# Weights of q, k and v of the third scan in three fp32r products, u's parts kept in one place, and both directions of a second-scan level in one VectorE instruction

## What is computed

```python
u = rmsnorm(h, norm_mix_g[l])
(s_z, s_xbc, s_dt, g_q, g_f, g_i, g_g, m_q, m_k, m_v, m_i, m_f, m_o, gates) = split(u @ w_in[l])
y_ssd = ssd_branch(s_z, s_xbc, s_dt)            # first scan, 16 heads, both directions
y_hg  = hgrn2_branch(g_q, g_f, g_i, g_g)        # second scan, 8 heads of 128 channels, both directions
y_ml  = mlstm_branch(m_q, m_k, m_v, m_i, m_f, m_o)   # third scan, 8 heads, both directions
merged = gate0 * (y_ssd @ w_br_ssd) + gate1 * (y_hg @ w_br_hg) + gate2 * (y_ml @ w_br_ml)
h = h + merged @ w_out
u = rmsnorm(h, norm_ffn_g[l]);  h = h + (silu(a) * v) @ w_down      # a, v from a convolution of u @ w_up
h = h + (p @ w_ple) * sigmoid(h @ w_ple_gate)
```

## Time and profile before

| | us |
|---|---|
| median of 3 runs (lowest, highest) | 2100.21 (2099.66, 2102.2) |
| span of the profiled execution, first to last instruction | 2098.0 |
| TensorE matmuls busy | 1965.0 (94%) |
| VectorE busy | 1271.7 (61%) |
| ScalarE busy | 932.0 (44%) |
| POOL busy | 31.4 (1%) |

### The profile page before, as it was taken

The page is one execution under the profiler, slowest core; times in us unless marked ns, Lnnn a source line. Parts: engine busy times, 40 slices in busy tenths (PEclk is TensorE's granted clock), DMA queues, the critical chain, the costliest instruction groups (busy, mean ns, idle before and its releaser), DMA issues.

```text
span 2098.0 us, 45360 instructions
## 1 busy us (share of the span) xinstructions
PE 1965.0 (94%) x19452; PEld 1719.3 (82%) x19452; DVE 1271.7 (61%) x2183; ACT 932.0 (44%) x1166; POOL 31.4 (1%) x62
## 2 busy tenths in 40 slices
PE   8999999999999999999999999999999996777776
PEld 7998869999999999988689999999977764444444
DVE  6887879489688567896895796786435311111111
ACT  5544655574565445546455754664422310111011
POOL 0000000000000000000000000000000000000000
PEclk9999999999999999999999999999999998999988
DMA  6555344445455554654434544555777899999997
GB/s 238 183 206 188 130 161 143 170 181 187 167 183 184 205 184 160 218 202 147 176 129 154 201 161 163 186 186 190 264 321 277 353 427 429 429 428 429 429 429 318
DMA packets 60269, 498.86 MB, mean 238 GB/s; under 512 B 7152, under 2 KB 7280, under 8 KB 12240
## 3 DMA queue, kind: packets, MB, share of 16 engines
q1 hardware_dynamic: 54864, 479.57, 59.5%
q0 software_dynamic: 4384, 14.49, 2.1%
q10 hardware_dynamic: 864, 2.49, 0.4%
HBM read 495.38 MB, written 1.15 MB: 237 GB/s over the span
## 4 chain that ended last, share of the span: by engine, by line
PE 72%; DMA 15%; DVE 8%; ACT 3%; issue 1%; ACTq 0%; SPq 0%; DVEq 0%
PE bank L1063 28%; DMA arena<-stream 15%; PE bank L1068 14%; PE bank L1073 4%; PE bank L1670 3%; PE bank L1051 3%; PE bank L1357 3%; PE bank L1002 3%; PE bank L990 2%; PE bank L1056 1%; DVE ring_r L2742 1%; PE bank L1105 1%; PE bank L1704 1%; PE bank L1649 1%; PE bank L1460 1%
## 5 line engine op out<-in xcount | busy, mean ns | idle before, releaser
L2742 DVE TENSOR_TENSOR ring_r<-ring,weights_and_u_split 128x2048 fp32r<-128x2048 f32 x88 | 201.5, 2291 | 76.5 <-ACT weights_and_u_split L2050 72.8
L1068 PE MATMUL bank<-weights_and_u_split,ring_r 128*128 128x256 f32 x1880 | 246.4, 283 | 0.0
L1068 PEld LDWEIGHTS bank<-weights_and_u_split,ring_r 128*128 128x128 f32 x1880 | 234.8, 192 | 0.0
L1063 PE MATMUL bank<-weights_and_u_split,hidden_and_weights_high 128*128 128x256 f32 x1664 | 211.5, 284 | 0.0
L1063 PEld LDWEIGHTS bank<-weights_and_u_split,hidden_and_weights_high 128*128 128x128 f32 x1664 | 203.6, 192 | 4.8 <-issue 4.3
L2050 ACT ACTIVATE weights_and_u_split<-ring 128x2048 fp32r<-128x2048 f32 x88 | 167.6, 1906 | 53.8 <-PE bank L1068 42.4
L3103 DVE COPY arena<-bank 128x128 f32<-128x128 f32 x32 | 9.3, 292 | 287.1 <-PE bank L1688 287.1
L1670 PE MATMUL bank<-arena 128*32 128x256 f32 x1504 | 108.5, 439 | 62.3 <-DMA arena<-stream 61.3
L2742 DVE TENSOR_TENSOR ring_r<-ring,hidden_and_weights_high 128x2048 fp32r<-128x2048 f32 x64 | 146.2, 2287 | 28.6 <-ACT hidden_and_weights_high L2050 28.5
L2239 ACT ACTIVATE arena<-bank 64x256 f32<-64x256 f32 x32 | 12.1, 377 | 314.1 <-PE bank L1670 314.1
L1670 PEld LDWEIGHTS bank<-arena 128*32 128x32 f32 x1504 | 54.7, 122 | 111.0 <-issue 51.5
(11 more groups left out here) (487 smaller groups left out, 3630.1 us busy)
## 6 DMA issues: line engine op xcount, KB each, us to landing
ring<-stream SPq DMA_DIRECT2D x267, 1024.0 KB, 4.8
arena<-stream SPq DMA_DIRECT2D x55, 2048.0 KB, 25.7
ring<-stream SPq DMA_DIRECT2D x26, 2048.0 KB, 26.7
arena<-stream SPq DMA_DIRECT2D x19, 1024.0 KB, 10.9
arena<-rows_scratch POOLq DMA_DIRECT2D x48, 256.0 KB, 4.2
place_of_rows<-stream SPq DMA_DIRECT2D x2, 1024.0 KB, 6.0
place_of_parameters<-stream SPq DMA_DIRECT2D x2, 1024.0 KB, 8.0
h<-x_d ACTq DMA_DIRECT2D x4, 256.0 KB, 4.9
```

The lines of the kernel that those rows point to most:

```text
L1063: pe.matmul(bank[:, c * S:(c + 1) * S], whi[k][:, c * P:(c + 1) * P], yhi[k] if xx is None else xx[:, k, :], start=(sub == 0 and c == part ...
L1068: mm = pe.matmul(bank[:, c * S:(c + 1) * S], wlo[k][:, c * P:(c + 1) * P], yhi[k] if xhi is None else xhi[:, k, :], start=False, stop=(end ...
L2742: tt(scan_high_or_low(k, ring_r[:, POS[k] % RING, :]), scan_high_or_low(k, w), high(k).bitcast(F32), ALU.subtract)\
```

## The change

Three edits. The 12 units of mq, mk and mv join the split units (`FIRST_SCAN`): their high parts go to two places in turn (`WMQ`), mv is multiplied in the form of hi, and the splits of mq and mq + 1 stand in the last steps of the first scan, that of mq + 2 ahead of `hlog` 0, those of mq + 3 to mq + 11 in steps 2 to 10, the high part at the head of the step and the low part at its end. u's high part has a place of its own (130, in an arena longer by 16 chunks), its low part is in u_r; both stay from the norm on, so `u_high`, `u_low`, `xsplit` 1 and what waited for them go, and the later xsplits are renumbered. The room comes from the scratch of the dynamic DMA queue, set to 2048. And in hgA and hgB the two directions' instructions become one, through a view (`both`) that steps from one direction's halves to the other's. The modulation row of pair 0 is kept in rstd's first half.

```diff
@@ -104,7 +104,8 @@
 EARLY = [n for n, kind in enumerate(KINDS) if kind in ("z", "xbc", "hf", "hq", "hi", "hg")]
 MID = [n for n, kind in enumerate(KINDS) if kind in ("gh", "gm", "bh", "bm", "out")][2:]
 SCAN = [n for n, kind in enumerate(KINDS) if kind in ("mo", "gs")] + [OF["gh"], OF["gh"] + 1]
-SPLIT = EARLY + SCAN + MID + [n for n, kind in enumerate(KINDS) if kind in ("up", "down", "pleg")]
+FIRST_SCAN = [n for n, kind in enumerate(KINDS) if kind in ('mq', 'mk', 'mv')]
+SPLIT = EARLY + FIRST_SCAN + SCAN + MID + [n for n, kind in enumerate(KINDS) if kind in ("up", "down", "pleg")]
...
-        WHI, UHI, HIDHI = (58, 66, 74), 82, 102
-        WHI1, ULO1 = (106, 114, 122), 90
+        WHI, UHI, HHI, HIDHI = (58, 66, 74), 130, 82, 102
+        WHI1, WMQ = (106, 114, 122), (138, 66)
         WSCAN = (HF, 122, HF, 122, HF, HF, HF, HF, 42, 0)
-        WHI2, UHI2, YHHI, YMHI, MGHI = (42, 74, 0), 16, (114, 116, 118, 96), 24, 114
+        WHI2, YHHI, YMHI, MGHI = (42, 74, 0), (114, 116, 118, 96), 24, 114
...
-        ADA_L = (66, 96, 16)
+        ADA_L = (None, 96, 16)
...
+            if i < len(FIRST_SCAN):
+                return WMQ[i % 2]
+            i -= len(FIRST_SCAN)
...
-            if i < 18:
+            if i < 20:
...
-            if i < 18:
+            if i < 20:
...
         mq = OF["mq"]
-        sched += [("hsig", 0), ("products", mq), ("products", mq + 1), ("ssd_norm", 0), ("hsig", 1), ("read", mq),
-                  ("hclamp", 0), ("ssd_add", 0), ("hlog", 0), ("ssd_log", 0), ("hsilu", 0), ("read", mq + 1), ("hgK", 0)]
+        sched += [("hsig", 0), ("products", mq), ("products", mq + 1), ("ssd_norm", 0), ("hsig", 1), ("read", mq), ("hi", mq + 2),
+                  ("hclamp", 0), ("ssd_add", 0), ("lo", mq + 2), ("hlog", 0), ("ssd_log", 0), ("hsilu", 0), ("read", mq + 1), ("hgK", 0)]
         gh, gs, mo = OF["gh"], OF["gs"], OF["mo"]
         for i in range(2, 24):
+            if i + 1 < 12:
+                sched.append(("hi", mq + i + 1))
             if i in (17, 19, 21):
                 sched.append(("hi", gs + i - 15))
             elif i == 23:
                 sched.append(("hi", gh))
             elif 11 <= i <= 15:
                 sched.append(("hi", mo + i - 11 if i < 15 else gs))
-            if i == 12:
-                sched.append(("u_low", 0))
...
                 sched.append(("msig", 0))
+            if i + 1 < 12:
+                sched.append(("lo", mq + i + 1))
...
-            if i == 10:
-                sched.append(("u_high", 0))
...
         sched += [("products", gh), ("split", gh + 1), ("products", gh + 1), ("mlA", 0), ("mlA", 1), ("split", gh + 2), ("read", gh),
-                  ("xsplit", (1, range(4))), ("hi", gh + 3), ("read", gh + 1)]
+                  ("hi", gh + 3), ("read", gh + 1)]
...
-                elif kind == "hi":
-
-                    late = (n - OF["hi"]) % 2
+                elif kind in ("hi", "mv"):
+
+                    late = (n - OF[kind]) % 2
                     whi, wlo = (x.rearrange("p (k m) -> p k m", k=4) for x in (high(n), ring_r[:, POS[n] % RING, :]))
-                    uhi, ulo = chunks_r(UHI, KC), chunks_r(ULO1, KC)
+                    uhi, ulo = chunks_r(UHI, KC), u_r
...
-                elif kind == "mv":
-
-                    late = (n - OF["mv"]) % 2
-                    wt = slot.rearrange("p (k m) -> p k m", k=4)
-                    for i in range(T):
-                        use = USE[n - late + i]
-                        if not late:
-                            pe.wait_ge(freed[use % GBANKS].sem, freed[use % GBANKS].at(lay, use // GBANKS))
-                        for k in range(4):
-                            mm = pe.matmul(G[use % GBANKS][:, :], u[:, 4 * late + k, i * P:(i + 1) * P], wt[:, k, :],
-                                           start=(not late and k == 0), stop=(late == 1 and k == 3), skip_group_check=True)
...
                     elif kind == "pleg":
-                        xhi, xlo = chunks_r(UHI, KC), chunks_r(HLO, KC)
-                    elif n in SCAN:
-                        yhi = [scan_u(k, 1)[:, 0, :] for k in range(KC)]
-                        xhi, xlo = None, u_r
-                    elif kind in ("gh", "gm"):
-                        xhi, xlo = chunks_r(UHI2, KC), u_r
+                        xhi, xlo = chunks_r(HHI, KC), chunks_r(HLO, KC)
                     else:
-                        xhi, xlo = chunks_r(UHI, KC), chunks_r(ULO1, KC)
+                        xhi, xlo = chunks_r(UHI, KC), u_r
...
-                    if n == OF["gh"] + 1:
-                        act.wait_ge(uhi_ok.sem, uhi_ok.at(lay, 12))
...
+                    elif k == OF["mq"] + 1:
+                        act.wait_ge(arg_ok.sem, arg_ok.at(lay, SSD_H))
+                    elif k == OF["mo"]:
+                        act.wait_ge(hqk.sem, hqk.at(lay, 9))
...
-                elif kind == "u_high":
-                    act.wait_ge(hqk.sem, hqk.at(lay, 9))
-                    for j in range(4):
-                        act.activation(scan_u(2 * j, 2).rearrange("p c s -> p (c s)"), u[:, 2 * j:2 * j + 2, :].rearrange("p c s -> p (c s)"),
-                                       ACT.Copy).then_inc(uhi_ok.sem, 1)
...
+            def both(first, b, forth, back, m):
+
+                x = flat(first, 22)
+                start, step = 4 * b * S + forth, 8 * S + back - forth
+                return x[:, start:start + 2 * step].rearrange("p (d r) -> p d r", d=2)[:, :, 0:4 * S]\
+                    .rearrange("p d (n m) -> p d n m", m=m)
...
-                elif kind == "u_low":
-                    dve.wait_ge(unit_done.sem, unit_done.at(lay, POS[last("mv")] + 1))
-                    for j in range(4):
-                        dve.wait_ge(uhi_ok.sem, uhi_ok.at(lay, 4 + j + 1))
-                        x, low = (t[:, 2 * j:2 * j + 2, :].rearrange("p c s -> p (c s)") for t in (u, u_r))
-                        ins = tt(low, x, scan_u(2 * j, 2).bitcast(F32).rearrange("p c s -> p (c s)"), ALU.subtract)
-                    ins.then_inc(ulo_ok.sem, 1)
...
                         q = m // 2
-                        st.done(tt(half(pf, q, 1), half(pf, q, 1), half(pf, q, 0)[:, :, q - 1:q].broadcast_to([P, 2 * n, q]), ALU.add))
-                        st.done(tt(half(sbw, q, 0), half(sbw, q, 0), half(sbw, q, 1)[:, :, 0:1].broadcast_to([P, 2 * n, q]), ALU.add))
+                        far = both(HF, b, q, 0, 2 * q)[:, :, :, 0:q]
+                        near = both(HF, b, q - 1, q, 2 * q)[:, :, :, 0:1]
+                        st.done(tt(far, far, near.broadcast_to([P, 2, 2 * n, q]), ALU.add))
                         st.wait()
-                    ek = flat(e + 4, 4)
-                    tt(half(ek, m, 0), half(pf, m, 0)[:, :, m - 1:m].broadcast_to([P, n, m]), half(pf, m, 0), ALU.subtract)
-                    tt(half(ek, m, 1), half(sbw, m, 1)[:, :, 0:1].broadcast_to([P, n, m]), half(sbw, m, 1), ALU.subtract)\
-                        .then_inc(hargs.sem, 1)
+                    ek = flat(e + 4, 4).rearrange("p (n d m) -> p d n m", d=2, m=m)
+                    edge = both(HF, b, m - 1, m, 2 * m)[:, :, :, 0:1]
+                    tt(ek, edge.broadcast_to([P, 2, n, m]), both(HF, b, 0, m, 2 * m)[:, :, :, 0:m], ALU.subtract).then_inc(hargs.sem, 1)
...
                     tt(flat(e, 4), flat(e, 4), flat(HQ + 4 * b, 4), ALU.mult)
-                    ek = flat(e + 4, 4)
-                    tt(half(ek, m, 0), half(ek, m, 0), half(flat(HK + 4 * b, 4), m, 0), ALU.mult)
-                    tt(half(ek, m, 1), half(ek, m, 1), half(flat(HK + 8 + 4 * b, 4), m, 1), ALU.mult).then_inc(hqk.sem, 1)
+                    ek = flat(e + 4, 4).rearrange("p (n d m) -> p d n m", d=2, m=m)
+                    tt(ek, ek, both(HK, b, 0, m, 2 * m)[:, :, :, 0:m], ALU.mult).then_inc(hqk.sem, 1)
...
-    nc = _bacc.Bacc("TRN2", target_bir_lowering=False, num_devices=1)
+    nc = _bacc.Bacc("TRN2", target_bir_lowering=False, num_devices=1, dynamic_dma_scratch_size=2048)
```

More of the change, by code:

```diff
@@ L267, in program @@
         as_r, at = {}, 0
-        for name, first, n in (("hidden_low", 0, 42), ("scan_weights_high", 42, 16), ("weights_and_u_split", 58, 40), ("hidden_and_weights_high", 102, 28)):
+        for name, first, n in (("hidden_low", 0, 42), ("scan_weights_high", 42, 16), ("weights_and_u_split", 58, 40), ("hidden_and_weights_high", 102, 28), ("u_high_and_scan_weights_high", 130, 16)):
             if first > at:
@@ L789, in program @@
             if n < down + 12 and (n - down) % 3 == 2:
-                sched.append(("xsplit", (5, [(n - down) // 3])))
+                sched.append(("xsplit", (4, [(n - down) // 3])))
             elif n >= pleg:
@@ L1375, in ada_cols2 @@
             def ada_cols2(n):
[L1376 removed]
+                ada_columns(DEPTH * PAIRS1 + n, PAIR_BANK[n][0], flat(ADA[n % 2], 2))
             def win(j):
@@ L2419, in item @@
                     for j in range(4):
-                        dve.wait_ge(uhi_ok.sem, uhi_ok.at(lay, 24 * k + j + 1))
```

(4 more changed lines are left out.)

70 lines of the change are left out of this document (31 added, 39 removed).

## The result

The changed kernel takes 2126.2 us (median of 4 runs, 2124.2 to 2126.6) against 2100.6 of the kernel before in the same session: ratio 1.0123, 95% interval [1.0111, 1.0135], 25.6 us slower. The forecast was 2112. The profiled execution has a span of 2123.9 us, so 25.9 of it can be looked for in the trace. Lines of hgA, hgB and the splits move: L2579 is hgA's addition, L2583 its argument, L2597 and L2599 hgB's two products, L2718 a low part, L2037 a high part, L2417 the copy of the modulation columns, L1101 TensorE's products for them, L994 a unit by token, L1247, L1258 and L1267 hgB on TensorE (tiles of 32, 64 and 128).

What follows compares the result with a forecast made beforehand. TensorE bounded steps 2 to 11 of the second scan, with VectorE's 18 us of room filled by the change. TensorE's saving is spent waiting and each of two layers ends 6.0 us later: +12.0, span 2110.0, runs 2112; range 2096 to 2122.

Steps and rivals of the forecast that it cites:

- TensorE's part: Swapping 8 q/k and 4 v units to three products saves TensorE 16.4 us a layer, 33 us in all.
- VectorE's part: Up to A(11): ten low parts +22.0, u's old one -2.4, merges -1.5; work 67.5 to 85.6 us.
- Waits that remain: VectorE waiting for ScalarE in the second scan: 1.3, 2.2, 1.3 and 0.3 us, 5.1 in all; A(11) at 312.1.
- The 0.3 for exponentials in step 8: VectorE waits 0.3 us or so for exponentials 7, behind hlog(1), its tables, a bank read and a high part.
- its gather goes through another buffer: The gather of modulation, moved to a different buffer, was priced at nothing.
- The tail: From mq+10's low part at about 300.6: A(12) at 322.3 (+7.0), hgB(14) at 348.5 instead of 342.5.
- All that follows is TensorE's: After hgB(14), the bs unit and all behind it keep TensorE busy without a gap, starting 6.0 us later.
- Rival (c): TensorE's clock falls in its waits in the layers: +3 us a layer, runs 2118, at most 2130; chance 0.12.
- (a): Each merge saves 0.16 us, 2.8 us a layer less: +3.2, runs 2107; chance 0.15 with its neighbours.
- (b): VectorE's queue closes up, its 5.1 us of waits vanish: 2096, or 2090 with merges at 0.16; chance 0.13.

Runs made afterwards that it cites:

- e4: Changed kernel with the copy of the modulation columns moved behind the sum of the logarithms: 2115.0 us, ratio 1.0078 to the kernel before.
- e1: Kernel before with only the merged directions (one VectorE instruction for both): 2097.8 us, ratio 0.9988 to the kernel before.
- e2: Changed kernel with the two directions in two instructions again: 2130.5 us, ratio 1.0146 to the kernel before.
- e11: Changed kernel with 16 overwritten products filling TensorE's waits ahead of each of hgB(2) to hgB(6): 2128.6 us, ratio 1.0136 to the kernel before.
- e13: Changed kernel with five more fp32 products at the start of the second block: 2127.7 us, one run.
- e14: Changed kernel with ten more fp32 products at the start of the second block: 2128.2 us, one run.
- e3: Changed kernel with the third scan's q, k and v units in plain fp32 again, merges kept: 2096.2 us, ratio 0.9983 to the kernel before.
- e7: e3 with the four v units (mq+8 to mq+11) in three products and the logarithms' sum earlier: 2099.2 us, ratio 0.9997 to the kernel before.
- e9: e3 with four spread units (mq+5, mq+7, mq+9, mq+11) in three products: 2100.7 us, ratio 1.0008 to the kernel before.
- e12: e3 with two units of v (mq+9, mq+11) in three products: 2092.2 us, ratio 0.9967 to the kernel before.

## Why the prediction was wrong

The sign was right, and so was the mechanism, VectorE full and TensorE waiting for it. The size was half of what came: +12 forecast, +25.6 measured, above the range's 2122. Two steps failed: the list of waits that remain, which lacked the wait of the copy (9.6 us), and the claim that all behind the scan is TensorE's (4.4 us, whose cause is open).

- **TensorE's part** (16.4 us a layer saved and spent waiting): right in kind, a little too large. A split q or k unit at full speed takes 5.95 us from its start to hgB, with its neighbours as in the scan (322.21 to 328.16 in e4, a unit of mo in the same form), against 7.1 plain, and v 5.65 against 7.0 to 7.1: 1.15 and 1.4 saved where I had 1.3 and 1.5, some 15 us a layer. Most of it came back as records at the lower clock: busy time up to the second group of `ho` fell by 4.3. As TensorE waits anyway, the error in the saving costs little; its waits were 0.9 to 2.1 us and there was none from 284.1 to 299.2, where I had 2 to 2.7 in nearly every step.
- **VectorE's part** (10 low parts of 2.20, merges of 0.07): right in its prices; e1 and e2 speak for that of the merges. That A(11) starts at 312.24 in e4 against 312.1 is in part luck: VectorE's work up to there is 84.4 us instead of 85.6, and its idle time 6.4 instead of 5.1, with 0.88 us for hgB(6) and 0.39 for hgB(9) that I hadn't listed.
- **Waits that remain**: three right to 0.2 us. The 0.3 for exponentials in step 8 isn't there; ScalarE's work of that place comes back as TensorE's wait of 1.64 us for a bank in the changed kernel. The failing step is here. The list was of ScalarE's work alone. I looked at what stands behind each waiting instruction, but of the modulation I said only that its gather goes through another buffer, "nothing". The copy of its columns waits for TensorE, in VectorE's queue, ahead of a low part. In the kernel before it waited too, in time that VectorE had to spare; TensorE's busy time hid it. With TensorE late through VectorE, that cover was gone: 9.6 us.
- **The tail**: right in its working, from the low part of mq+10 on (at 300.2 in e4, forecast 300.6): +6.0 a layer in e4, and from A(12) to hgB(14) 26.4 us against the 26.2 forecast.
- **"All that follows is TensorE's"**: right for the rest of the layer, wrong for the second block, which adds 4.4 us in the changed kernel. Its cause is open.
- **Rival (c)**, the clock: it did fall, to 0.92 in 221 to 322 where I had named 0.95 as the mark. Its price in the layers is 1.6 + 2.5 = 4.1 us, not far from the 6 of the rival, but all of it behind one wait, and nothing up to A(7), where the short waits of nearly every step are. **(a)** falls with e1 and e2. **(b)** falls with the waits at the start, which were all there.

9.6, 4.4 and 11.9 make 25.9, the difference of the spans.

## What to carry to other kernels

When a change makes another engine the bound, look again at every instruction in that engine's queue that waits for the old bound: waits that were hidden by slack now stand ahead of critical work, and moving one 0.16 us copy back by two items of the list was worth some 10 us here. Work is best moved from a full engine to one with gaps one piece at a time, into the gaps that lie in front of a wait for the full engine: against the all-plain kernel, two units of v in three products won 4 us, four or five lost 3 to 5, twelve lost 30. An idle share is not room.

## What the runs showed of the hardware

- TensorE's granted clock was 0.90 from 221.4 to 306.9 in the changed kernel, where it waited 0.9 to 2.1 us in most steps and once 4.04; from 237 to 281 it was 0.92, and 1.00 in e11, where products filled the waits. The lower clock cost time only where TensorE was the one waited for.
- Two fp32 tensor_tensor instructions of 512 columns in one of 1024, with a broadcast edge and four dimensions, save 0.07 us by starts (1.21 to 1.14), in a queue that runs back to back. The whole kernels fit that (1.6 us in e1; 4.3 in e2, over about 60 merges), although durations say 0.16.
- The profiled executions of the changed kernel, e13 and e14, with the same code up to the second block, reach it up to 1.3 us apart; the argument of A(1) in e3, e7, e9 and e12, the same code up to there, lies between 226.8 and 228.2.
